# Four token tiles in the first output pass and two in the second, with all expert gates added by scatters

## What is computed

```python
v1, i1 = lax.top_k(s[..., 0, :], PEER_TOPK)
v2, i2 = lax.top_k(s[..., 1, :], PEER_TOPK)
cand = (v1[..., :, None] + v2[..., None, :])
cv, ci = lax.top_k(cand, PEER_TOPK)
expert = e1 * N_KEYS + e2
gate = jax.nn.softmax(cv, axis=-1)
pre = jnp.einsum('tkd,td->tk', expert_u[it], xt)
act = jax.nn.gelu(pre, approximate=False) * gt
out = jnp.einsum('tk,tkd->td', act, expert_v[it])
```

## Time and profile before

| | |
|---|---|
| median of 3 runs | 3867.58 us |
| the profiled execution | 3880.33 us |
| its span in the trace | 3878.8 us |
| mean granted TensorE clock | 0.972 |
| busy, share of the span | TensorE 94%, weight loads 81%, VectorE 69%, ScalarE 32%, GpSimd 48% |
| chain that ended last | TensorE 27%, GpSimd 16%, VectorE 7%, DMA 5%, issue 5% |

### The profile page before, as it was taken

The page is one execution under the profiler, slowest core; times in us unless marked ns, Lnnn a source line. Parts: engine busy times, 40 slices in busy tenths (PEclk is TensorE's granted clock), DMA queues, the critical chain, the costliest instruction groups (busy, mean ns, idle before and its releaser), DMA issues.

```text
span 3878.8 us, 55417 instructions
## 1 busy us (share of the span) xinstructions
PE 3628.0 (94%) x19324; PEld 3137.7 (81%) x19324; DVE 2680.8 (69%) x5241; ACT 1248.0 (32%) x1831; POOL 1850.6 (48%) x1496
## 2 busy tenths in 40 slices
PE   8989799998998899999999999999999995799999
PEld 6854488887876678899999999999777884578887
DVE  5443377775222348658888999997997662589897
ACT  3013343442111221233333333333334331333333
POOL 1024122231100106868888888678888888212220
PEclk9989899999999999999999999999999997899999
DMA  3249500001220133469899899885889995899997
GB/s 117 97 164 398 211 20 19 9 19 69 77 73 11 38 113 92 83 201 282 284 286 281 279 282 283 274 283 175 275 267 278 295 284 100 301 372 400 382 391 267
DMA packets 349345, 788.63 MB, mean 203 GB/s; under 512 B 110112, under 2 KB 218656, under 8 KB 315296
## 3 DMA queue, kind: packets, MB, share of 16 engines
q1 hardware_dynamic: 210208, 451.28, 34.7%
q0 software_dynamic: 139008, 336.01, 27.6%
HBM read 643.09 MB, written 144.05 MB: 203 GB/s over the span
## 4 chain that ended last, share of the span: by engine, by line
PE 27%; POOL 16%; DVE 7%; DMA 5%; issue 5%; DVEq 1%; ACT 1%; SPq 0%; POOLq 0%; ACTq 0%
PE peer_ps L2128 17%; POOL gates_d L2107 13%; PE peer_ps L2219 5%; PE peer_ps L2142 4%; DMA peer_hid<-gates_d 4%; DMA peer_gat<-gates_d 2%; POOL peer_gates L2102 2%; DVE peer_acc L2541 1%; POOL late_rows L2087 1%; DVEq L2435 1%; PE peer_ps L2165 1%; DVE peer_ul L2422 1%; ACT peer_uh L2315 0%; DVE peer_rows L2526 0%; DVE peer_al L2560 0%
## 5 line engine op out<-in xcount | busy, mean ns | idle before, releaser
L2107 POOL DMA_INDIRECT gates_d<-peer_gates,peer_idx x768 | 1201.2, 1564 | 339.3 <-issue 184.8
L2128 PE MATMUL peer_ps<-high,peer_uh 128*128 128x384 f32 x2048 | 522.0, 335 | 10.8 <-DVE peer_ul L2422 5.0
L2128 PE MATMUL peer_ps<-low,peer_uh 128*128 128x384 f32 x2048 | 520.7, 335 | 0.0
L2128 PE MATMUL peer_ps<-high,peer_ul 128*128 128x384 f32 x2048 | 520.4, 334 | 0.0
L2128 PEld LDWEIGHTS peer_ps<-high,peer_uh 128*128 128x128 f32 x2048 | 369.4, 188 | 14.9 <-issue 7.9
L2128 PEld LDWEIGHTS peer_ps<-high,peer_ul 128*128 128x128 f32 x2048 | 370.6, 188 | 0.0
L2128 PEld LDWEIGHTS peer_ps<-low,peer_uh 128*128 128x128 f32 x2048 | 370.6, 188 | 0.0
L2219 PE MATMUL peer_ps<-peer_vh,peer_ah 128*128 128x512 f32 x1026 | 321.5, 395 | 22.5 <-DVE peer_al L2560 22.4
L2087 POOL DMA_INDIRECT late_rows<-in_expert_uv,peer_idx x108 | 142.1, 1316 | 402.3 <-DVE peer_acc L2541 349.8
L2219 PE MATMUL peer_ps<-peer_vh,peer_al 128*128 128x512 f32 x1026 | 318.3, 391 | 0.0
L2219 PE MATMUL peer_ps<-peer_vl,peer_ah 128*128 128x512 f32 x1026 | 318.2, 391 | 0.0
(11 more groups left out here) (473 smaller groups left out, 7680.8 us busy)
## 6 DMA issues: line engine op xcount, KB each, us to landing
peer_raw<-in_expert_uv SPq DMA_DIRECT2D x170, 512.0 KB
gates_d<-mla_zeros POOLq DMA_DIRECT2D x128, 512.0 KB
hidden_d<-peer_hid SPq DMA_DIRECT2D x128, 384.0 KB, 3.7
peer_raw<-in_expert_u SPq DMA_DIRECT2D x86, 512.0 KB, 5.4
first_raw<-in_expert_uv SPq DMA_DIRECT2D x86, 512.0 KB, 5.1
peer_act_in<-hidden_d SPq DMA_DIRECT2D x171, 192.0 KB, 5.2
peer_gat<-gates_d SPq DMA_DIRECT2D x171, 192.0 KB, 6.0
first_raw<-in_expert_u SPq DMA_DIRECT2D x42, 512.0 KB
```

The lines of the kernel that those rows point to most:

```text
L2107: pool.indirect_dma_start(gates_flat, bass.IndirectOffsetOnAxis(ap=idx[:, n, k:k + 1], axis=0), gates[:, n, k:k + 1], None, compute_op=ALU ...
L2128: last = nc.tensor.matmul(ps[i][:, a, 0:HD], w[:, cols], x[:, kc, a * HD:(a + 1) * HD], start=(kc == 0 and w is uh[i % 2] and x is high), ...
```

## The change

The passes have four and two tiles: `PASSES` is 0, 1, 2, 3 and then 4, 5. So a block of pass 0 has 24 matmuls and a block of pass 1 has 12, and pass 0 needs 32 units of gates in place of 24. Piece 6, the running sums, their buffers and GpSimd's additions are gone: all scatters of heads 1 to 7 add. Gathers are timed by `ROWS_BY`, which is interpolated: 148 over units 7 to 27 as before, none until unit 33, then 76 (in place of 28) until the middle of unit 47, and 32 (in place of 80) after the scatters. VectorE takes a group of two rows every 3 slots in pass 0 (8.5 before) and every 7 slots in pass 1 (3 before).

```diff
-PASSES = ((0, 1, 2), (3, 4, 5))
-EARLY_SLOTS, PASS_SLOTS = 148, 28
+PASSES = ((0, 1, 2, 3), (4, 5))
+EARLY_SLOTS, PASS_SLOTS = 148, 76
...
-SUMMED = 4
+ROWS_BY = ((7, 0), (28, EARLY_SLOTS), (33, EARLY_SLOTS), (47.5, EARLY_SLOTS + PASS_SLOTS))
...
-            steps = ((0,), (1, 2, 3), (4,), (5, 6))
+            steps = ((0,), (1, 2, 3), (4,), (5,))
...
-            return OUT + 13 + (g * 17) // 2 if g < PASS_SLOTS // GROUP else OUT + NK + 3 + 3 * (g - PASS_SLOTS // GROUP)
+            return OUT + 13 + 3 * g if g < PASS_SLOTS // GROUP else OUT + NK + 3 + 7 * (g - PASS_SLOTS // GROUP)
...
-            if i < 7:
-                return 0
-            if i < 31:
-                return min(EARLY_SLOTS, EARLY_SLOTS * ((i - 7) * TOPK + k + 1) // (21 * TOPK))
-            return EARLY_SLOTS + (min(PASS_SLOTS, PASS_SLOTS * ((i - 31) * TOPK + k + 1) // (14 * TOPK)))
+            done = i + (k + 1) / TOPK
+            return int(np.interp(done, [x for x, _ in ROWS_BY], [y for _, y in ROWS_BY]))
...
-                    if summed(n):
-                        nc.gpsimd.tensor_tensor(gates[:, n, k:k + 1], gates[:, n, k:k + 1],
-                                                earlier_sum[:, tile - PASSES[1][0], head - 1, k:k + 1], ALU.add
-                                                ).then_inc(sum_made, 1)
-                        sums_made += 1
-                        pool.wait_ge(sum_made, sums_made)
                     pool.indirect_dma_start(gates_flat, bass.IndirectOffsetOnAxis(ap=idx[:, n, k:k + 1], axis=0),
                                             gates[:, n, k:k + 1], None,
-                                            compute_op=ALU.bypass if head == 0 or summed(n) else ALU.add
+                                            compute_op=ALU.add if head else ALU.bypass
                                             ).then_inc(added[tile % 4], 16)
...
-                if piece == 6 and summed(n):
...
-                    nc.vector.tensor_tensor(same, e.unsqueeze(2).broadcast_to([P, TOPK, m]),
-                                            prior_e[:, t, 0:head, :].rearrange("p h k -> p (h k)").unsqueeze(1)
-                                            .broadcast_to([P, TOPK, m]), ALU.is_equal)
...
-                    nc.vector.tensor_reduce(earlier_sum[:, t, head - 1, :], same, AX.X, ALU.add).then_inc(idx_ready, 1)
```

More of the change, by code:

```diff
@@ L1811, in unit_pieces @@
         if slot < WT - 1:
-            steps = ((0, 1, 2, 3, 4), (5, 6))
+            steps = ((0, 1, 2, 3, 4), (5,))
         elif slot < WT + NK:
-            steps = ((0,), (1, 2, 3), (4,), (5, 6))
+            steps = ((0,), (1, 2, 3), (4,), (5,))
         else:
-            steps = ((0,), (1,), (2,), (3,), (4,), (5, 6))
+            steps = ((0,), (1,), (2,), (3,), (4,), (5,))
         for i, pieces in enumerate(steps):
@@ L1862, in peer_stage @@
                                              for i in range(HOME_ROWS, RING_IN)]
-            prior_e, prior_g = (home.enter_context(nc.sbuf_tensor(f"peer_{x}", [P, len(PASSES[1]), SUMMED, TOPK], F32))
-                                for x in ("prior_e", "prior_g"))
         val = raw
@@ L1877, in peer_stage @@
         tok_i, tok = st.sb("tok_i", [P, NT], I32), st.sb("tok", [P, NT])
[L1878 to L1880 removed]
+        nmax, gsum = st.sb("nmax", [P, 1]), st.sb("gsum", [P, 1])
         w_stored, w_taken, s_mm, s_ready, keys_ready = [st.sem(f"w_stored{i}") for i in range(2)], st.sem("w_taken"), st.sem(
@@ L1928, in ahead @@
             return {OUT - 2: 0, OUT - 1: 1}.get(b)
-        def summed(n):
-            head, tile = units[n]
-            return tile in PASSES[1] and 0 < head < SUMMED
         def scatters(head, tile):
@@ L2091, in _ @@
             nc.gpsimd.iota(tok_i[:, :], [[P, NT]], base=0, channel_multiplier=1).then_inc(iota_ready, 1)
-            turn, sums_made = 0, 0
+            turn = 0
             for i, n in enumerate(dense):
@@ L2483, in choose @@
                     dve.drain()
[L2484 to L2490, removed]
+                    tile = units[n][1]
@@ L2491, in choose @@
+                    nc.vector.scalar_tensor_tensor(out=flat_e[:, :], in0=e12[:, 0, :], scalar=float(NK),
+                                                   in1=e12[:, 1, :], op0=ALU.mult, op1=ALU.add)
+                    nc.vector.tensor_scalar(gates[:, n, :], gexp[:, :], gsum[:, :], None, ALU.mult)
                     dve.drain()
-                    if kept:
-                        last = nc.vector.tensor_copy(prior_g[:, t, head, :], gates[:, n, :])
                     if tile >= DENSE:
-                        last = nc.vector.tensor_copy(idx[:, n, :], e)
+                        nc.vector.tensor_copy(idx[:, n, :], flat_e[:, :]).then_inc(idx_ready, 1)
@@ L2496, in choose @@
                     else:
-                        last = nc.vector.tensor_scalar(idx[:, n, :], e, float(T), tok[:, tile:tile + 1], ALU.mult,
-                                                       ALU.add)
-                    if not summed(n):
-                        last.then_inc(idx_ready, 1)
-                if piece == 6 and summed(n):
-                    head, t = units[n][0], units[n][1] - PASSES[1][0]
-                    m = head * TOPK
-                    e = prior_e[:, t, head, :]
-                    same = work[:, 0:TOPK * m].rearrange("p (k j) -> p k j", j=m)
-                    nc.vector.tensor_tensor(same, e.unsqueeze(2).broadcast_to([P, TOPK, m]),
-                                            prior_e[:, t, 0:head, :].rearrange("p h k -> p (h k)").unsqueeze(1)
-                                            .broadcast_to([P, TOPK, m]), ALU.is_equal)
-                    dve.drain()
-                    nc.vector.tensor_tensor(same, same,
-                                            prior_g[:, t, 0:head, :].rearrange("p h k -> p (h k)").unsqueeze(1)
-                                            .broadcast_to([P, TOPK, m]), ALU.mult)
-                    dve.drain()
-                    nc.vector.tensor_reduce(earlier_sum[:, t, head - 1, :], same, AX.X, ALU.add).then_inc(idx_ready, 1)
@@ L2516, in row_hidden @@
+                        nc.vector.tensor_scalar(idx[:, n, :], flat_e[:, :], float(T), tok[:, tile:tile + 1], ALU.mult,
+                                                ALU.add).then_inc(idx_ready, 1)
             def row_hidden(slot):
```

1 line of the change is left out of this document (removed).

## The result

The changed kernel takes 3941.49 us, the median of 3 runs (3938.76 to 3943.18), against 3867.58 before. The ratio, taken against the runs of the kernel before that belong to it, is 1.0174, with a 95% interval of [1.0149, 1.0198]. That is 67 us; the two medians differ by 74. It is slower, as forecast, but by about twice the 36 us of the sum. The profiled execution has a span of 3941.6 us, 62.8 more than before; its mean granted clock is 0.966.

A forecast was written before the change was run, and what follows sets the result against it. GpSimd's scatters were taken to set when gates are ready. Non-matmul time 56 + 7 + 2 + 35 + 51 = 151 us against 114, tail -1.3, made +36 on 3867.58: 3904 us; own range 3872 to 3936, stretched to 3852 to 3948.

The forecast's parts named there:

- Start of pass 0: End of first stage: gates need 32 units, so pass 0 starts at 2754, +56 us, plus 7 us at the lower clock.
- Running sums: GpSimd's 144 scatters of tiles 3 to 5 become adds: 29 to 43 us more for GpSimd, contained in other terms.
- The seam: Between the passes: scatters done at 3422, landed at 3425, so the gap of 62.7 us goes; 2 us left.
- Pass 0: First pass, four tiles: 35 us of stalls in all, with 20 and 80 as bounds.
- Rival C: In pass 0, DMA is the bound as well: every block 0.35 us longer, +45 us, 3949; chance 0.11.
- Pass 1: Second pass, two tiles: 3.1 us a block against 2.72, 51 us in all, bounds 10 and 85 us.
- For the landing I take 5.4: Landing time of the gates load in pass 1: 5.4 us, between 6.2 among gathers and 4.3 without.
- The ring: Pass 1's loads in three sets: load q waits for the split of q - 3; three blocks take 9.7 us.
- the signs: Expected in the trace: among others, pass 1 in about 400 us and no idle time over 5 us at 3500.
- Rival A: Pass 1 keeps TensorE's pace, 2.72 us a block: saves the ring's 45 us, 3859; chance 0.17.
- B: Rival: GpSimd is in time for pass 0, so 63 us fall away, 3841; chance 0.06.
- D: Rival: the wait between passes stays if an add costs over 2.38 us; at 2.5 about 3935; chance 0.06.

The follow-up runs named there:

- Run 2: The changed kernel without the scatters of heads 6 and 7 for tiles 0 to 3; ratio 1.0010, 63 us less than the changed kernel.
- run 1: The kernel before, passes still three and three tiles, with running sums removed so GpSimd adds heads 1 to 7; ratio 1.0043, +17 us.
- run 3: The changed kernel with the last 32 looked-up rows neither gathered nor worked on; ratio 0.9986, 73 us less than the changed kernel.
- run 10: The changed kernel with four sets of tables in pass 1 and without the last 32 looked-up rows; ratio 0.9945.
- run 5: The changed kernel with the second gather of a pair held back some four blocks in pass 1; ratio 1.0112, 24 us less.
- run 6: The changed kernel with four sets of tables in place of three in pass 1; ratio 1.0106, 26 us less than the changed kernel.
- Run 9: The changed kernel with four sets of tables, gathers apart, normalization one tile in a block and, in pass 1, one row in a slot; ratio 0.9992.
- run 8: The changed kernel with four sets of tables and the first four tiles' normalization spread one tile in a block; ratio 1.0090.

## Why the prediction was right, and where it was short

The direction and the list of terms were right; one term was half its size. In the order of the sum, on the profiled execution:

1. *Start of pass 0*, +56 and 7 cold: the first matmul is at 2750.51 against 2698.20, +52.3 (forecast 2754). Run 2 shows that it is GpSimd and nothing else. That the first stage could become shorter was costed at nothing, because GpSimd would hide it; it became 7.6 us shorter, and GpSimd hid it.
2. *Running sums*, 29 to 43 us of GpSimd: 27 us in run 1, over the units where the edit acts. Right in kind, a little high. Only 12.3 us of it reached the seam there, since GpSimd was ahead for other reasons.
3. *The seam*, gap goes: right, with 2 us allowed and none seen. The last scatter ended at 3436.6, 15 us later than forecast, and the slack held.
4. *Pass 0*, 35 us: from 2750.5 to 3475.35 are 725 us against 704 pure (697 of blocks, 7 of residual), so 21, with the 7 of the cold restart in them; TensorE waited 11 us in all. Too high by 21. Rival C, DMA as its bound, is false: 100% busy at 331 GB/s.
5. *Pass 1*, 51 us: from 3475.35 to the end of its matmuls at 3933.3, 458.0 us against 352.5 pure (349 of blocks, 3.5 of residual), are **105 us**. This is the step that failed: "For the landing I take 5.4, between the two rows", and so 3.1 us a block. The ring was named rightly. Without rows its sum comes out: 0.95 + 5.0 + 2.65 = 8.6 us for three blocks, where run 3 turned in 8.5, and a fourth set saved 16 us there (run 10). The 5.4 was right as well, as a median: 5.5. But a ring stops at its slowest landing and not at the median. The loads right behind a pair of gathers took 9 us, one turn in seven blocks, and apart they cost 24 us less (run 5). Added to that, VectorE's row work falls into the same turn (run 6), and the clock falls after each gap. How much is which: in 3550 to 3800, 40.1 of the 250 us were idle, and the 813 matmuls of the other 209.9 would have needed 184 at the pace of the earlier trace rows (442 in 100 us), so some 26 us went to the slow clock. The prediction knew the clock's fall from the earlier trace rows and charged it only at the restart of pass 0.

In all, 52 + 21 + 105 = 178 us are not matmul, where the prediction had 151. Pass 1 was 54 us too low and the other terms together 27 too high (73 for 100), so the total missed by 27 on the profiled execution only because two errors worked against each other; that part is luck. Another 11 us of the miss on the medians, 38 in all, come from a step of the sum: it let the 12.7 us by which the profiled execution of before was longer than its median carry over, and after it was 1.7.

The measured 3941 lies outside the forecast's own range of 3872 to 3936. It is inside 3852 to 3948 only because that was stretched toward rival C, which did not come true. Two of the signs also failed: pass 1 was to take about 400 us and took 458, and no idle time over 5 us was to stand at 3500, where the normalization left 8.4.

Against the kernel before, the 62.8 us between the two spans add up so: +52.3 at the start, -6.3 of stalls in pass 0, -62.7 at the seam, +80.9 in pass 1, -1.4 at the tail. The change moved the wait for gates from the seam to the start, and what it lost is pass 1.

Rival A (pass 1 keeps TensorE's pace) needed a landing under 4.6 us among gathers, and the median alone was 5.5; B (GpSimd in time) and D (the wait at the seam stays) are refuted by the 59.92 us of idle time and by the seam.

The Trainium skill, "DMA: Bandwidth & Descriptors", Specifications, gives 358 GB/s as a core's limit to memory. Run 9 at 359 GB/s with a DMA share of 1.00 looks like it, yet run 1, with three tiles in a pass, moved 401 at 1.03 for 50 us (3550 to 3600): by the trace the limit of run 9 is not one of bytes alone. What it is was not tried.

## What to carry to other kernels

When a change shortens the work per block, the cover of a ring shrinks with it while the landing does not; check the ring against the slowest landing in a period, behind the largest burst that shares the DMA engines, not against the median. Two releases close together make two transfers close together: with a fourth set of buffers, issuing and computing one by one and a spread normalization won 70 us here with no work removed, 26 of them by the set alone. Look also at where a wait goes that a change removes: here it stood again, as long as before, in another place. And charge each gap of several microseconds on TensorE with the slow clock behind it; a ring deep enough to break one long gap into short ones wins that part even where idle time stays.

## What was not expected of the hardware

- The granted clock fell to 0.51 for some 6 us behind a TensorE gap of 4.13 us, and such gaps came again every seven blocks: the mean was 0.90 over the 250 us of 3550 to 3800, with ten waits of 3.2 to 4.2 us. It was 0.96 and 0.97 in the two kernels with one or two waits of 3.1 to 3.3 us there (runs 5 and 8), and 1.00 in the one with waits of up to 2.1 (run 6).
- A 128 KB load, the third of its set, issued 1.6 us behind the second of two gathers of 1 MB, landed after 9 us, where the median beside it was 5.5, and 5.0 with no gathers at all.
- An adding scatter cost GpSimd 1.56 us plus 0.30 of issue when VectorE stood still and 1.81 to 1.85 plus 0.30 among other work: 0.19 us more than a bypass with its own small addition.
